# Norm roots through logarithm and exponential, and a head and a tail cut into feature blocks, in a two-layer decoder trunk

## The chip, the cores and the metric

The kernel runs on one core of a Trainium2 chip. Four engines work beside each other and meet only at semaphores: TensorE multiplies matrices and writes its sums to PSUM, ScalarE evaluates functions and copies, VectorE does elementwise arithmetic, and GpSimd does one elementwise operation here. SyncE's queue issues nearly all DMAs. The metric is device time in microseconds (us), from the start to the end of the program on the core. Lower is better.

## The reference

One inference step of a trunk of two layers, for a prompt of 1,024 tokens and 8 single-token samples, so 1,032 token columns of 1,024 features. A layer is, in float32:

```
x += RMSNorm_post([window attention ; HGRN2 recurrence](RMSNorm_pre(x) @ w_in) @ w_o)
x += RMSNorm_post(cross attention to 256 memory tokens(RMSNorm_pre(x)))
x += RMSNorm_post(gated MLP(causal depthwise conv(RMSNorm_pre(x) @ w_up)) @ w_down)

RMSNorm(x) = x * rsqrt(mean(x*x) + 1e-6) * g
memory keys, values = RMSNorm(mem_prompt) @ w_xk, w_xv
HGRN2 output: o = o * rsqrt(mean(o*o, over 128) + 1e-6) * gn * silu(gate), for each of 4 heads
```

It returns the 1,032 columns of x and the new caches.

## The kernel before, in words

Features lie on the 128 partitions in KT = 8 blocks, tokens in the free dimension. `xT` is the residual stream, `Y` the output of a sub-layer, `rs` the scale of a norm for each token. The tokens are cut into three chunks, of 344 columns in the mixer's projections and in the MLP, and of 384, 384 and 264 in the two stages between.

A float32 product is made of three fast ones (`mm3`, lines 256 to 260): each operand is split into a rounded high part and the remainder, as `hh` and `hl` for the activations and `w_hi` and `w_lo` for the weights. ScalarE makes the high parts, VectorE the low part of activations (L1094, L1103, L1639, L2499), and GpSimd the low part of a weight slab of 128x1024 (L243). From the end of the output projection to the query projection VectorE does this for 13 slabs per layer (L252, `low_slab`). Two raw and three split slabs are held, so each load waits for a split and each split waits for TensorE to have used an older slab. A "unit" is one slab times one chunk: 8 blocks of 3 matmuls.

There is no scheduler. The order on each engine is the order of the code, written out by hand in functions named `sync`, `gpsimd`, `tensor`, `scalar` and `vector`, and an instruction that waits holds back everything behind it on its engine. The stages of a layer:

1. Mixer (`stage_mixer`): 22 slabs by 3 chunks. The units of later slabs are spread as "hooks" through the recurrence of four heads. Each head ends with its norm: TensorE sums the squares of the output, 8 matmuls of one column at L944, ScalarE takes the square root (L1079), VectorE the reciprocal of 8 values per partition (L1317) and multiplies an identity by them (L1318), TensorE spreads these to all partitions (L951), VectorE multiplies (L1326). In the last head VectorE also applies the rotary embedding (`rope`, L1191 to L1193).
2. Window attention and the memory's projection (`stage_window`): 16 units `memory(f)` beside 16 groups of attention. `memory(0)` waits for all 8 blocks of the memory's low part `ml` (L637).
3. Output and query projection (`stage_output_query`), 4. cross attention (`stage_cross_ffn`), 5. the MLP. Its last two slabs run together with the norm after it (class `End`). In layer 0 that norm runs into the mixer of layer 1, in layer 1 into `stage_last`, which writes x out.

A norm of a chunk: squares (ScalarE), their sum over features (a matmul against `ones`), `Sqrt` (ScalarE, L299, L980, L1538, L1970, L2340), `RECIPROCAL` (VectorE, L1116, L1615, L1648, L1990, L2018, L2485, L2508), and for a post-norm a multiplication of the whole chunk (L1622, L1994, L2487) and the residual, which multiplies by the gain and adds to `xT` (L1629, and in `End` L2004: one instruction for each of the 8 blocks).

The start (`stage_start` and the first lines of the mixer): the DMA queue loads the first slab, then chunk 0 of x, the second slab, chunks 1 and 2, the constants and the memory, and after them the third slab. ScalarE and VectorE split chunk 0 in 8 blocks each, and the first unit waits for the last block.

## Time and profile before

| | us |
|---|---|
| median of three runs | 3418.66 (3417.93 to 3419.36) |
| profiled execution, its own time | 3425.52 |
| its span, first to last instruction | 3423.7 |
| TensorE busy in matmuls | 3237.8 (95%) |
| VectorE busy | 2308.0 (67%) |
| ScalarE busy | 1173.6 (34%) |
| GpSimd busy | 686.8 (20%) |

The mean granted clock of TensorE is 0.983 of full speed. Busy time of a matmul counts from its start to its modelled end, and neighbours overlap, so the times at which matmuls start say more than their lengths. An idle time in brackets at the end of a row is how long the engine had nothing before it, and the arrow names what it waited for.

### The profile page before, as it was taken

What the parts mean: (1) busy time and instruction counts of PE and PEld (TensorE: products, weight loads), DVE (VectorE), ACT (ScalarE), POOL (GpSimd) and SP (SyncE); (2) the same over time, 40 slices, a digit from 0 to 9 for tenths busy, and PEclk for the clock granted to TensorE, in tenths of its full rate; (3) what the DMA queues carried; (4) which work ended last, traced back from release to release, by engine and by line L of the source; (5) the groups of instructions that cost most, each with busy time, mean ns of one, the idle gap of its engine ahead of it and who ended that gap; (6) DMA issues with size and microseconds to landing.
All of it is one profiled execution on the core that took longest, in us unless ns stands there. A gap on an engine that the chain in (4) does not pass through costs nothing. (4 is left out here: it accounts for less than half of the span.)

```text
span 3423.7 us, 51853 instructions
## 1 busy us (share of the span) xinstructions
PE 3237.8 (95%) x21872; PEld 3075.0 (90%) x21872; DVE 2308.0 (67%) x3413; ACT 1173.6 (34%) x1849; POOL 686.8 (20%) x274
## 2 busy tenths in 40 slices
PE   7999889899899999999989998898999999999997
PEld 7998769788799999999879987798887999999996
DVE  6776782834677767676787776737355777777776
ACT  5442363434522222222344424533344222121212
POOL 1111131012322222222111111310133222222220
PEclk9999999999999999999999999999999999999998
DMA  5112233213411111111121122332053111111111
GB/s 179 45 39 69 71 94 124 74 43 143 175 44 50 44 50 44 50 44 50 49 83 39 51 63 77 112 112 72 28 192 127 44 56 39 55 44 50 44 54 52
DMA packets 80135, 245.87 MB, mean 72 GB/s; under 512 B 7968, under 2 KB 32800, under 8 KB 76064
## 3 DMA queue, kind: packets, MB, share of 16 engines
q1 hardware_dynamic: 79616, 242.50, 21.1%
q8 instruction: 173, 2.83, 0.3%
q14 instruction: 58, 0.48, 0.0%
q10 hardware_dynamic: 288, 0.06, 0.0%
HBM read 214.20 MB, written 23.04 MB: 69 GB/s over the span
## 5 line engine op out<-in xcount | busy, mean ns | idle before, releaser
L258 PE MATMUL ps<-hh,w_hi 128*128 128x344 f32 (+2 forms) x4320 | 1418.2, 328 | 84.5 <-DVE w_lo L252 27.9
L259 PE MATMUL ps<-hl,w_hi 128*128 128x344 f32 (+2 forms) x4320 | 1391.3, 322 | 0.0
L260 PE MATMUL ps<-hh,w_lo 128*128 128x344 f32 (+2 forms) x4320 | 1391.1, 322 | 0.0
L243 POOL TENSOR_TENSOR w_lo<-w_raw,w_hi 128x1024 fp32r<-128x1024 f32 x270 | 686.6, 2545 | 2674.3 <-ACT w_hi L235 2674.3
L258 PEld LDWEIGHTS ps<-hh,w_hi 128*128 128x128 f32 x4320 | 822.5, 190 | 113.1 <-issue 53.9
L259 PEld LDWEIGHTS ps<-hl,w_hi 128*128 128x128 f32 x4320 | 822.1, 190 | 3.1 <-issue 0.9
L260 PEld LDWEIGHTS ps<-hh,w_lo 128*128 128x128 f32 x4320 | 822.3, 190 | 0.0
L2608 DVE TENSOR_TENSOR Y<-Y,ps 128x344 f32<-128x344 f32 x912 | 433.1, 513 | 155.7 <-PE ps L260 155.7
L235 ACT ACTIVATE w_hi<-w_raw 128x1024 fp32r<-128x1024 f32 x296 | 310.6, 1052 | 440.0 <-PE ps L260 381.7
L2407 ACT ACTIVATE f_c<-f_u,cT 128x1032 f32<-128x1032 f32 (+1 forms) x92 | 111.4, 1213 | 635.0 <-DVE f_u L2573 628.4
L259 PE MATMUL ps<-f_glo,w_hi 128*128 128x344 f32 x960 | 308.0, 321 | 0.0
L260 PE MATMUL ps<-f_ghi,w_lo 128*128 128x344 f32 x960 | 307.9, 321 | 0.0
L258 PE MATMUL ps<-f_ghi,w_hi 128*128 128x344 f32 x960 | 306.0, 319 | 0.0
L2581 DVE SCALAR_TENSOR_TENSOR f_c<-f_u,cT,f_c 128x1024 f32<-128x1024 f32 x172 | 225.2, 1309 | 98.7 <-ACT f_c L2407 95.6
L258 PEld LDWEIGHTS ps<-f_ghi,w_hi 128*128 128x128 f32 x960 | 181.2, 189 | 0.0
L260 PEld LDWEIGHTS ps<-f_ghi,w_lo 128*128 128x128 f32 x960 | 180.5, 188 | 0.0
L259 PEld LDWEIGHTS ps<-f_glo,w_hi 128*128 128x128 f32 x960 | 180.3, 188 | 0.0
L2573 DVE TENSOR_TENSOR f_u<-ps,rs 128x1032 f32<-128x1032 f32 x86 | 105.7, 1230 | 63.5 <-PE ps L260 63.3
L2583 DVE SCALAR_TENSOR_TENSOR f_c<-f_cache,cT,f_c 128x8 f32<-128x8 f32 x172 | 124.1, 722 | 6.2
L1603 DVE TENSOR_TENSOR oq_acc<-oq_acc,oq_sq 128x384 f32<-128x384 f32 (+1 forms) x84 | 43.3, 515 | 96.3 <-ACT oq_sq L1528 92.4
L2423 ACT ACTIVATE f_ghi<-f_c 128x1032 fp32r<-128x1032 f32 x42 | 44.9, 1069 | 149.2 <-DVE f_c L2589 149.2
L1126 DVE TENSOR_TENSOR Y<-ps,rs 128x344 f32<-128x344 f32 x120 | 60.0, 509 | 47.6 <-PE ps L260 47.4
(357 smaller groups left out, 3717.5 us busy)
## 6 DMA issues: line engine op xcount, KB each, us to landing
w_raw<-in_w_stream SPq DMA_DIRECT2D x296, 512.0 KB, 3.5
out_y_cols<-xT SPq DMA_DIRECT2D x9, 1376.0 KB, 6.2
xT<-out_y_cols SPq DMA_DIRECT2D x2, 4128.0 KB, 13.6
mem_keys<-in_cache_mem_k SPq DMA_DIRECT2D x6, 1024.0 KB, 5.2
Y<-in_cache_mem_k SPq DMA_DIRECT2D x6, 1024.0 KB, 7.8
mem_values<-in_cache_mem_v SPq DMA_DIRECT2D x6, 1024.0 KB, 8.0
mem_keys<-in_cache_mem_v SPq DMA_DIRECT2D x6, 1024.0 KB, 7.8
xT<-in_x_cols SPq DMA_DIRECT2D x3, 1376.0 KB, 11.3
```

The source lines that it names most:

```text
L235: nc.scalar.activation(w_hi[:, SLOT[m], :], w_raw[:, m % RR, :], ACT.Copy).then_inc(hi_done, 1)
L243: nc.gpsimd.tensor_tensor(w_lo[:, SLOT[m], :], w_raw[:, m % RR, :], w_hi[:, SLOT[m], :].bitcast(F32), ALU.subtract).then_inc(lo_done["pool ...
L258: nc.tensor.matmul(out, whi, mhi, start=start, stop=False)
L259: nc.tensor.matmul(out, whi, mlo, start=False, stop=False)
L260: return nc.tensor.matmul(out, wlo, mhi, start=False, stop=stop)
L1126: nc.vector.tensor_tensor(dst[:, cols(c)], ps[:, u % 3, 0:CH], rs[:, cols(c)], ALU.mult)\
L2407: nc.scalar.activation(C[:, h, at], U[:, h, 2 + at.start:2 + at.stop], ACT.Identity, bias=cT[:, l, 3, col:col + 1], scale=cT[:, l, 2, col: ...
L2423: nc.scalar.activation(gh[:, j % 2, :], C[:, 1, :], ACT.Copy).then_inc(f_gh, 1)
L2573: nc.vector.tensor_tensor(tokens3(U[:, h, 2:2 + T]), ps[:, 3 * h:3 * h + 3, 0:CH], tokens3(rs[:]), ALU.mult).then_inc(f_up, 1)
L2581: dve_c(nc.vector.scalar_tensor_tensor(c[:, 0:SEQ], U[:, h, t:t + SEQ], w, c[:, 0:SEQ], ALU.mult, ALU.add))
L2583: dve_c(nc.vector.scalar_tensor_tensor(c[:, SEQ:T], ca[:, col, t, :], w, c[:, SEQ:T], ALU.mult, ALU.add))
L2608: nc.vector.tensor_tensor(y, y, b, ALU.add).then_inc(f_y, 1)
```

## The change

Roots. Everywhere a norm took `Sqrt` on ScalarE and `RECIPROCAL` on VectorE, ScalarE now makes the inverse root by two activations, `Ln` of the mean plus epsilon and `Exp` of minus half of that (`inverse_root`). The second waits for the first. VectorE only waits. The table set with both functions is loaded by name (`load_log_exp`) at the start, behind sigmoids and silus, and at the end of each MLP.

Head norms. The squares of a head are summed by `ones` as the stationary operand over 512 columns at a time, so the sum arrives on all partitions, and ScalarE takes the inverse root of 1,024 columns. The 8 one-column matmuls, the identity product and the second broadcast go. In the order of ScalarE, two exponentials of the next head now come ahead of the root.

End of an MLP. ScalarE multiplies `Y` by the gain in place, block by block, behind each square (`gained`). The multiplication by `rs` goes in two halves of 4 blocks, and the residual is a plain addition of 4 blocks at a time. x is written out in halves in `stage_last`, where ScalarE's root of chunk 1 now stands before three blocks of chunk 2.

Start. Chunk 0 of x arrives in two DMAs of 4 blocks, ScalarE and VectorE wait for the half that they need, VectorE and TensorE wait block by block, and the first mean comes behind the second unit. `memory(0)` waits for its operand block by block.

```diff
+        def load_log_exp():
+            nc.scalar.preload_act_table_set("natural_log_exp_and_others")
+        def inverse_root(out, log, total, n, ready):
+            act_c(nc.scalar.activation(log, total, ACT.Ln, bias=epst[:], scale=1.0 / n))
+            nc.scalar.activation(out, log, ACT.Exp, scale=-0.5).then_inc(ready, 1)
...
+                def x_here(self, eng, c, k=KT - 1):
+                    if c == 0 and k < KT // 2:
+                        eng.wait_ge(x_half, 16)
+                    else:
+                        eng.wait_ge(x_in[c], 16)
...
-                sp.dma_start(xT[chunk(0)], io["x_cols"][chunk(0)]).then_inc(x_in[0], 16)
+                sp.dma_start(xT[:, 0:4, 0:CH], io["x_cols"][:, 0:4, 0:CH]).then_inc(x_half, 16)
+                sp.dma_start(xT[:, 4:KT, 0:CH], io["x_cols"][:, 4:KT, 0:CH]).then_inc(x_in[0], 16)
...
                             for k in range(KT):
+                                if f == 0:
+                                    pe.wait_ge(s["m_lo"], k + 1)
...
-                        pe.wait_ge(s["m_lo"], KT)
                         memory(0)
...
-                            if end and w == 0:
-                                pe.wait_ge(end.s["hl"], KT * c + k + 1)
+                            if w == 0:
+                                pe.wait_ge((end.s if end else s)["hl"], KT * c + k + 1)
...
                         unit(0)
+                        unit(1)
                         mean_of_x(0)
-                        for u in (1, 2, 3):
+                        for u in (2, 3, 4):
...
-                        for c in range(NB):
-                            nc.tensor.matmul(ps[:, BB, c:c + 1], att[:, P * c:P * c + P], ones[:, 0:1], start=True, stop=True)
+                        for h in range(2):
+                            nc.tensor.matmul(ps[:, BB + h, :], ones[:], att[:, 512 * h:512 * h + 512], start=True, stop=True)
...
-                        unit(hook_units(r, 11)[0])
-                        pe.wait_ge(s["spread"], r + 1)
-                        for h in range(2):
-                            last = nc.tensor.matmul(ps[:, BB + h, :], ones[:], RT[:, 512 * h:512 * h + 512],
-                                                    start=True, stop=True)
-                        last.then_inc(s["cast"], 1)
-                        for u in hook_units(r, 11)[1:]:
-                            unit(u)
+                        hook(r, 11)
...
-                        nc.scalar.activation(sq8[:], ps[:, BC, 272:272 + NS], ACT.Sqrt, bias=epst[:],
-                                             scale=1.0 / P).then_inc(s["root"], 1)
                         if more:
                             exp_level(r + 1, 1)
                             exp_level(r + 1, 2)
+                        act.wait_ge(s["mean"], r + 1)
+                        inverse_root(two(RT), two(RT), pair(BB), P, s["root"])
+                        inverse_root(sq8[:], sq8[:], ps[:, BC, 272:272 + NS], P, s["root"])
...
-                        nc.vector.tensor_tensor(two(y[:, 0:SEQ]), two(y[:, 0:SEQ]), pair(BB), ALU.mult)\
-                            .then_inc(s["normed"], 1)
+                        nc.vector.tensor_tensor(y[:, 0:SEQ], y[:, 0:SEQ], RT, ALU.mult).then_inc(s["normed"], 1)
...
                             nc.scalar.activation(self.slot(e, k), Y[:, k, cols3(c)], ACT.Square).then_inc(self.s["sq"], 1)
+                            nc.scalar.activation(Y[:, k, cols3(c)], Y[:, k, cols3(c)], ACT.Copy,
+                                                 scale=gT[:, l, G_POST_FFN + k:G_POST_FFN + k + 1]).then_inc(self.s["gained"], 1)
...
-                        dve_c(nc.vector.reciprocal(rs[:, cols3(c)], rs[:, cols3(c)]))
...
+                        for h in range(2):
+                            at = (slice(None), slice(4 * h, 4 * h + 4), cols3(c))
+                            nc.vector.tensor_tensor(Y[at], Y[at], over_heads(rs[:, cols3(c)], 4), ALU.mult)\
+                                .then_inc(self.s["norm"], 1)
...
+                            nc.vector.tensor_tensor(xT[at], xT[at], Y[at], ALU.add).then_inc(self.s["x"], 1)
...
+                    for h in range(2):
+                        sp.wait_ge(end.s["x"], 2 * c + h + 1)
+                        at = (slice(None), slice(4 * h, 4 * h + 4), slice(CH * c, CH * c + CH))
+                        sp.dma_start(io["y_cols"][at], xT[at]).then_inc(y_out, 16)
```

VectorE at the end of a head, before. `hg_blast` holds the 8 roots, `xT` the spread scale, `Y<-ps,rs` is the evacuation of a unit:

```order
L1126 TENSOR_TENSOR Y<-ps,rs 128x344
L1317 RECIPROCAL hg_blast<-hg_blast 128x8
L1318 TENSOR_TENSOR xT<-ident,hg_blast 128x1024
L1320 RECIPROCAL hg_sq<-hg_sq 128x8
L1321 TENSOR_TENSOR Y<-Y,hg_sq 128x8
L1162 TENSOR_TENSOR hg_work<-hg_work,xT 128x512
L1164 TENSOR_TENSOR hg_work<-hg_work,xT 128x512
L1126 TENSOR_TENSOR Y<-ps,rs 128x344
L1326 TENSOR_TENSOR Y<-Y,ps 128x1024
```

The same place now:

```order
L1135 TENSOR_TENSOR Y<-ps,rs 128x344
L1171 TENSOR_TENSOR hg_work<-hg_work,xT 128x512
L1173 TENSOR_TENSOR hg_work<-hg_work,xT 128x512
L1328 TENSOR_TENSOR Y<-Y,hg_sq 128x8
L1135 TENSOR_TENSOR Y<-ps,rs 128x344
L1330 TENSOR_TENSOR Y<-Y,xT 128x1024
```

The reciprocals and the identity product are gone, and the two products of the next head stand ahead of the wait for the root. ScalarE at the same place, before (L1004 is the exponential of the next head's levels):

```order
L1075 ACTIVATE hg_work<-ps 128x1024
L1079 ACT_TABLE_LOAD
L1079 ACTIVATE hg_blast<-ps,epst 128x8
L1080 ACTIVATE hg_sq<-ps,epst 128x8
L1004 ACT_TABLE_LOAD
L1004 ACTIVATE hg_work<-hg_work 128x1024
L1004 ACTIVATE xT<-xT 128x1024
```

And now, where L1013 is that exponential:

```order
L1088 ACTIVATE hg_work<-ps 128x1024
L1013 ACTIVATE hg_work<-hg_work 128x1024
L1013 ACTIVATE xT<-xT 128x1024
L268 ACTIVATE xT<-ps,epst 128x1024
L269 ACTIVATE xT<-xT 128x1024
L268 ACTIVATE hg_sq<-ps,epst 128x8
L269 ACTIVATE hg_sq<-hg_sq 128x8
```

Two table loads have gone from here, and two activations of 1,024 columns have come, behind the exponentials. VectorE's last rows of the program, before:

```order
L1986 TENSOR_TENSOR Y<-Y,ps 128x344 x5
L1990 RECIPROCAL rs<-rs 128x344
L1994 TENSOR_TENSOR Y<-Y,rs 128x8x344
L2004 SCALAR_TENSOR_TENSOR xT<-Y,gT,xT 128x344 x8
L1990 RECIPROCAL rs<-rs 128x344
L1994 TENSOR_TENSOR Y<-Y,rs 128x8x344
L2004 SCALAR_TENSOR_TENSOR xT<-Y,gT,xT 128x344 x8
```

And now:

```order
L1984 TENSOR_TENSOR Y<-Y,ps 128x344 x5
L1993 TENSOR_TENSOR Y<-Y,rs 128x4x344 x2
L2004 TENSOR_TENSOR xT<-xT,Y 128x4x344 x2
L1993 TENSOR_TENSOR Y<-Y,rs 128x4x344 x2
L2004 TENSOR_TENSOR xT<-xT,Y 128x4x344 x2
```

Twenty rows of work have become thirteen. In the whole program ScalarE's order holds 64 table loads before and 44 now, and no norm root has one directly ahead of it.

## Rows read from the trace of the kernel before

**Rows 1.** The page, part 1: engine, busy us, share of the span, instructions.

```profile
PE 3237.8 (95%) x21872; PEld 3075.0 (90%) x21872; DVE 2308.0 (67%) x3413; ACT 1173.6 (34%) x1849; POOL 686.8 (20%) x274
```

**Rows 2.** Busy time of each engine by stretch; PEclk is the granted clock.

```profile
core 0: us, PE busy (x) PEld busy (x) DVE busy (x) ACT busy (x) POOL busy (x), PEclk, DMA share, GB/s
...
586.00:672.00 86.00, 70.74 (x423) 66.87 (x422) 72.20 (x100) 42.51 (x80) 0.00 (x0) 0.94 0.25 80
...
1671.00:1754.00 83.00, 66.92 (x324) 58.14 (x323) 71.37 (x92) 35.38 (x61) 10.11 (x4) 0.89 0.22 77
```

**Rows 3.** Groups in both mixers, PE: count, busy us, mean ns, idle before, releaser.

```profile
L944 PE MATMUL ps<-ones,hg_work 128*128 128x1 f32 x128 | 14.7, 245 | 0.0
```

**Rows 4.** The end of a head; start us, length, engine, line, idle before.

```profile
76.36 1.09 PE L901 MATMUL ps<-ident,Y 128*128 128x128 f32 x8 [0.95 <-DVE Y L1126]
...
215.92 1.88 PE L951 MATMUL ps<-xT,ones 128*128 128x512 f32 x4
...
219.20 2.02 PE L852 MATMUL ps<-hg_set 128*128 128x128 f32 x16 [0.42 <-DVE Y L1326]
...
214.13 1.06 ACT L1004 ACTIVATE hg_work<-hg_work 128x1024 f32<-128x1024 f32 x1
```

**Rows 5.** Output and query projection of layer 0, the same columns.

```profile
634.59 2.56 DVE L1648 RECIPROCAL rs<-oq_rt 128x384 f32<-128x384 f32 x1 [0.18 <-ACT oq_rt L1538]
...
641.51 0.44 PE L258 MATMUL ps<-hh,w_hi 128*128 128x384 f32 x1 [2.13 <-DVE w_lo L252]
...
645.68 1.80 DVE L1615 RECIPROCAL oq_rt<-oq_rt 128x264 f32<-128x264 f32 x1
...
653.76 0.69 PE L258 MATMUL ps<-hh,w_hi 128*128 128x384 f32 x1 [3.46 <-DVE w_lo L252]
```

**Rows 6.** The last head's end and the memory's first unit.

```profile
385.48 1.98 PE L951 MATMUL ps<-xT,ones 128*128 128x512 f32 x4 [1.80 <-DVE xT L1318]
...
401.70 1.28 ACT L542 ACT_TABLE_LOAD   x1
...
402.50 0.58 PE L258 MATMUL ps<-mem_hi,w_hi 128*128 128x256 f32 x1 [4.28 <-DVE mem_lo L637]
```

**Rows 7.** From the MLP of layer 0 into the mixer of layer 1.

```profile
1725.37 2.30 DVE L1990 RECIPROCAL rs<-rs 128x344 f32<-128x344 f32 x1
...
1733.61 3.98 DVE L2004 SCALAR_TENSOR_TENSOR xT<-Y,gT,xT 128x344 f32<-128x344 f32 x8
...
1733.84 1.49 PE L1928 MATMUL ps<-e_whole,ones 128*128 128x344 f32 x2 [3.82 <-DVE e_whole L2013]
```

**Rows 8.** The tail of the program.

```profile
3397.30 4.79 PE L1922 MATMUL ps<-e_squares,ones 128*128 128x344 f32 x16
...
3399.00 2.30 DVE L1990 RECIPROCAL rs<-rs 128x344 f32<-128x344 f32 x1 [0.99 <-ACT rs L1970]
...
3404.40 3.99 DVE L2004 SCALAR_TENSOR_TENSOR xT<-Y,gT,xT 128x344 f32<-128x344 f32 x8
...
3413.69 3.99 DVE L2004 SCALAR_TENSOR_TENSOR xT<-Y,gT,xT 128x344 f32<-128x344 f32 x8
```

**Rows 9.** The head of the program.

```profile
9.37 3.88 ACT L963 ACTIVATE hh<-xT,gT 128x344 fp32r<-128x344 f32 x8 [2.81 <-DMA xT<-in_x_cols]
...
13.39 6.09 DVE L1094 SCALAR_TENSOR_TENSOR hl<-xT,gT,hh 128x344 fp32r<-128x344 f32 x8 [8.88 <-ACT hh L963]
...
19.63 0.63 PE L258 MATMUL ps<-hh,w_hi 128*128 128x344 f32 x1 [19.63 <-DVE hl L1094]
...
24.40 1.06 ACT L235 ACTIVATE w_hi<-w_raw 128x1024 fp32r<-128x1024 f32 x1 [7.81 <-DMA w_raw<-in_w_stream]
...
25.53 2.39 POOL L243 TENSOR_TENSOR w_lo<-w_raw,w_hi 128x1024 fp32r<-128x1024 f32 x1 [8.87 <-ACT w_hi L235]
```

**Rows 10.** The page, part 6: DMA, KB each, median us to landing.

```profile
w_raw<-in_w_stream SPq DMA_DIRECT2D x296, 512.0 KB, 3.5
...
out_y_cols<-xT SPq DMA_DIRECT2D x9, 1376.0 KB, 6.2
```

More of the change, by code:

```diff
@@ L298, in root @@
                     act.wait_ge(s["mean"], 1)
[L299 removed]
+                    inverse_root(mrs[:], mrs[:], ps[:, 7, 0:NMEM], D, s["root"])
                 def scale(self, dve):
                     dve.wait_ge(s["root"], 1)
[L303 removed]
             def sync(sp):
@@ L810, in unit @@
                             wait_low(pe, m)
-                        if w < 3 and not end:
-                            pe.wait_ge(s["hl"], c + 1)
                         if u >= 3:
@@ L1198, in vector @@
                         end.tree(dve, 2)
-                        end.residual(dve, 1, range(KT))
+                        end.residual(dve, 1, (0, 1))
                         end.scale(dve, 2)
@@ L1205, in vector @@
                         end.tree(dve, 4)
-                        end.residual(dve, 2, range(KT))
+                        end.residual(dve, 2, (0, 1))
                         end.scale(dve, 4)
@@ L1533, in root @@
                         def root(i):
+                            kind, c = MEANS[i]
                             act.wait_ge(mean_ready, i + 1)
-                            if i >= 2:
-                                act.wait_ge(rt_used, i - 1)
-                            n = C3[MEANS[i][1]][1]
-                            nc.scalar.activation(rt[:, i % 2, 0:n], ps[:, 3, 0:n], ACT.Sqrt, bias=epst[:], scale=1.0 / D)\
-                                .then_inc(rt_ready, 1)
+                            if i >= 2 and MEANS[i - 2][0] == "post":
+                                act.wait_ge(rt_used, sum(k == "post" for k, _ in MEANS[:i - 1]))
+                            r = rt[:, i % 2, 0:C3[c][1]]
+                            inverse_root(r if kind == "post" else rs[:, cols(c)], r, ps[:, 3, 0:C3[c][1]], D, rt_ready)
                         def high(c):
@@ L1866, in stage_cross_ffn @@
                     EVENTS += [("pre", 0), ("post", 2), ("pre", 1), ("pre", 2)] if l + 1 < DEPTH else [("post", 2)]
-                    s = {n: sem(f"e_{n}") for n in ("sq", "sum", "root", "x", "hh", "hl", "rs", "norm", "whole", "tree", "mean")}
+                    s = {n: sem(f"e_{n}") for n in ("sq", "gained", "sum", "root", "x", "hh", "hl", "norm", "whole", "tree", "mean")}
                     added = 24 * (FT - 2)
@@ L2335, in root @@
                     def root(i):
+                        kind, c = MEANS[i]
                         act.wait_ge(s["mean"], i + 1)
-                        if i >= 2:
-                            act.wait_ge(s["rt_used"], i - 1)
-                        w = C3[MEANS[i][1]][1]
-                        nc.scalar.activation(rt[:, i % 2, 0:w], ps[:, mean_bank(i), 0:w], ACT.Sqrt, bias=epst[:], scale=1.0 / D)\
-                            .then_inc(s["root"], 1)
+                        if i >= 2 and MEANS[i - 2][0] == "post":
+                            act.wait_ge(s["rt_used"], sum(k == "post" for k, _ in MEANS[:i - 1]))
+                        r = rt[:, i % 2, 0:C3[c][1]]
+                        inverse_root(r if kind == "post" else rs[:, cols(c)], r, ps[:, mean_bank(i), 0:C3[c][1]], D, s["root"])
                     def high(c, ks):
@@ L2682, in scalar @@
                 end.scalar(act)
-                end.squares(act, 2, range(KT))
+                end.squares(act, 2, range(5))
                 end.root(act, 1)
+                end.squares(act, 2, range(5, KT))
                 end.root(act, 2)
@@ L2689, in vector @@
                 for c in (1, 2):
-                    end.normalise(dve, c)
-                    end.residual(dve, c, range(KT))
-                dve.wait_ge(end.s["x"], KT * NCH)
+                    end.reciprocal(dve, c)
+                    end.multiply(dve, c)
+                    end.residual(dve, c, (0, 1))
+                dve.wait_ge(end.s["x"], 2 * NCH)
             return Programs(sync, gpsimd, tensor, scalar, vector)
```

111 lines of the change are left out of this document (41 added, 70 removed).

## The prediction

> **What bounds the kernel now.** I read the engine shares first. TensorE is busy for 95% of the span [rows 1]. So a gain has to come from its own work or from the places where it stands still, and I listed its idle times above half a microsecond in the timeline, with what ended each. They sit in six kinds of places: the head, the ends of heads, the entry into the window stage, the stretch of the two projections, the norm between the layers, and the tail. In the projections VectorE is the busier engine, 72.20 of 86 us against TensorE's 70.74, and between the layers 71.37 of 83 against 66.92 [rows 2]. There TensorE waits for VectorE's chain, and a reciprocal in that chain is on the path. In the long MLPs TensorE has hardly an idle time, and nothing that the change does there reaches the path. All sums below are made against the profiled execution. Its span is 3423.7, its own time 3425.5, and the median of the runs 3418.7. A saving is taken over in full to the median.
>
> **Head ends, 8.4 us.** The 128 one-column matmuls cost 14.7 us of TensorE with no idle time ahead of them [rows 3], 1.84 for each of 8 heads. They go. The two 512-column matmuls (1.88 us) remain and move into their place, four microseconds earlier. They used to cover the evacuation of the last unit before the next head's transposes. That cover is gone. The price is shown where there never was a cover: 0.95 us before L901 after three evacuations [rows 4]. Here one is left, so I take 0.8. The wait of 0.42 before L852, which is for VectorE's multiplication of the norm, goes, since the bank is now free once ScalarE has read it. For a change of heads that is 1.84 + 0.42 - 0.8, about 1.4, and there are six: 8.4 us. ScalarE does more: two activations of 1,024 columns at about 1.06 each [rows 4] in place of two small ones, so the root is ready some 2.7 us after the sum. The unit behind the sum takes TensorE about 4 us and the transposes about 1.1 [rows 4], so this is hidden, by about 2.5 us. Were it not, TensorE would wait at L852 and everything behind it.
>
> **Last head and window, 7.2 us.** In each layer's last head the idle time of 1.80 before L951, behind VectorE's rotation and identity product, goes with the wait [rows 6], and 1.84 us of small matmuls too. But the last evacuation stands behind the last rotation, which waits for a DMA that VectorE starts when the rotation before it ends, and that order stays. I estimate 2.1 us there. Next, `memory(0)` started 4.28 us late, after all 8 low parts [rows 6]. Now it starts after the first. The table load of 1.28 us ahead of the window's first exponential goes. What is late next is the second group's probabilities on VectorE, and they leave 1.5 of these. So 3.6 per layer.
>
> *A rule beside it.* The load takes 1.28 us [rows 6]. The Trainium skill (ScalarE: Activation LUTs, What ACT_TABLE_LOAD costs) states that each switch of sets costs a drain of about 1.38 us besides, about 2.66 us in all. By that, the two loads on the window's path would be worth about 2.8 us more. The row has the load alone, nothing in the trace shows a drain, and I keep to the row.
>
> **Projections, 7.5 us.** TensorE waits for the low part of a slab three times here, 2.13 and 3.46 us being two of the waits [rows 5], and in front of the slabs stand three reciprocals, of which 2.56 and 1.80 us are two; the first has the length of the second. The first, for post-norm 0, gives nothing: the slab behind it is not split before then, and the largest wait of the stretch hangs on ScalarE's order. Those of post-norm 1 and pre-norm 0 move VectorE by 2.2 us, since the query's scale cannot come before TensorE's sum; the last adds 1.8. Less the new activation, TensorE meets the next wait (3.46) about 3.75 us earlier. Twice 3.75 is 7.5.
>
> **Cross attention, 0.5 us.** The samples' caches arrive by DMA and set the pace. Earlier normalisation takes a little contention from the splits of the slabs, about 0.8 per layer, and the last root, on which TensorE waits before the third chunk of the MLP's first slab, is longer by one activation, about 0.5. Net 0.5 in all.
>
> **Between the layers, 6 us.** Four reciprocals of 2.30 are on VectorE's chain, and two residuals of 3.98 [rows 7]. Multiplying a chunk takes 3.1 (from 3399.00 + 2.30 to 3404.40 [rows 8]), and an addition of the same 2,752 columns should take the same, 0.9 less than the eight fused ones. Against this, ScalarE now makes two activations for each block: at 0.485 a block (3.88 for 8) [rows 9] the eight squares of chunk 0 end about 3 us later. TensorE works on those for 4.8 us anyhow, so it loses about 1.9, and the first scale comes 1.5 later than with the reciprocal. Followed through the three sums, the start of the fourth unit comes 2 us earlier, the sum at 1733.84 about 4, and the last sum 6 to 8. I take 6.
>
> **Tail, 9 us.** From 3399.00 to the span's end VectorE and the last output are alone: 2.3 + 3.1 + 4.0, the same again, and 6.0 for the last DMA (3413.69 + 3.99 to 3423.7) [rows 8]. Now the root of chunk 1 is made before the last blocks arrive, so multiplication starts when the last addition ends, about 3398.0 (TensorE is done at 3397.30). Four pieces of 3.1 end at 3410.4. The root of chunk 2 needs TensorE's sum (3397.30 + 4.79 = 3402.1) and two activations, 3403.2, and the multiplication wants it at 3404.2: in time. A DMA of 512 KB lands in 3.5 us, one of 1,376 KB in 6.2 [rows 10], so 688 KB less save 2.1. The end is at 3410.4 + 3.9 = 3414.3. That is 9.4; I take 9, for ScalarE's longer rows.
>
> **Head, 2.3 us.** TensorE's first product was at 19.63, after 8 high parts (9.37, 3.88) and 8 low parts (13.39, 6.09) one after the other [rows 9]. With half of chunk 0 landed some 2 us sooner (half of 1,376 KB, by the price above) and a wait per block, it starts at about 9, when the first slab is split. That looks like 10 us, but the third slab lands at 24.40 and is split at 25.53 + 2.39 = 27.9 whatever happens before, because the DMA queue is unchanged. TensorE will do two units and stop. The third cannot start before that. What remains, estimated between 1 and 3, is 2.3 us; the cleared reciprocal of 2.30 keeps the fourth from waiting.
>
> *A rule beside it.* VectorE's low parts of chunk 0 took 6.09 us for 8 with a split on GpSimd beside them, against 3.98 for 8 fused instructions of that width between the layers [rows 9, 7]. The Trainium skill (SBUF - State Buffer, Who interferes with whom) calls the pair of ports that both use an exclusive lock for the whole instruction. By it, the low parts of chunk 1, which now start under the split at 25.53, wait for it, and the head's gain would shrink to about 1.
>
> **The rivals.**
> (a) The clock comes back too. Granted clock was 0.94 in the projections of layer 0 and 0.89 between the layers [rows 2], some 14 us of half speed's loss, behind stops that now get shorter; two thirds more of the kind lie elsewhere. If a third of it is returned, 8 to 10 us more: about 3368. For it: the low clock follows the stops. Against: most stops are only shortened, and the head gets a new one.
> (b) ScalarE is late. If squares with gains and the long roots each cost more than I allow, between the layers brings 1 and the head ends 3, the rest as above: 9 less of the gain and 2 to 4 at other roots, about 3390.
> (c) Slower than before. ScalarE's extra 2 us per head delays the split of a slab, and TensorE waits for slabs in place of norms. It decides once a split falls later than the start of its unit, more than 5 us after now; then each of 32 slabs in heads would cost up to 2 us, 64 less 41: about 3442. Against: ScalarE is idle for two thirds of the time there, and TensorE shows no wait for a split in the heads.
> (d) The change does not do what it says: table loads come back ahead of each `Ln`. The order of ScalarE shows 44 loads, none at a root, so little speaks for it. Price: 1.28 at some 40 roots, half of them on the path, 26 us: about 3403.
>
> **How the numbers follow.** 8.4 + 7.2 + 7.5 + 0.5 + 6 + 9 + 2.3 is 40.9, so 3418.7 becomes 3378. Chances: this case 0.60, (a) 0.16, (b) 0.18, (d) 0.03, (c) 0.03. Adding the bounds of the terms (tail 7 to 10, between the layers 3 to 9, head 1 to 3, head ends 5 to 10, the rest by a third either way), the range is 3364 to 3394, which takes in (a) and (b). A measurement of this kernel can tell 0.2%, about 7 us, from no change. Only (c) lies on the slow side, and little of (d) and of what I have not seen lies near no change: faster 0.96, same 0.01, slower 0.03.
>
> **What would show it.** Right: the last residual ends near 3370 of a span of about 3383, with an end 14 us after TensorE's last sum begins; L901 shows idle times of 0.6 to 0.9 at changes of heads and L852 none; the first product stands near 9, followed by a stop of about 8 us before the third slab; waits for slabs in the projections fall by some 4 us per layer. Wrong: the head shows 8 us or more of gain, TensorE waits for ScalarE's root at a change of heads, the clock is 1.00 where it was 0.89, or the sum of idle times between the layers has not fallen.

## The result, and the profile after

The changed kernel takes 3380.97 us (median of 4 runs, 3377.77 to 3383.46) against 3418.3 us of the kernel before on the same chip: a ratio of 0.9890, 95% interval 0.9873 to 0.9907. On the chip of the first experiments it came to 3379.54 us and 0.9877 (0.9863 to 0.9890). The forecast was 3378 with a range from 3364 to 3394. It held in its sum; several of its terms were off, and some of them cancel. One execution of one kernel below, heads as before, took 6381.9 us, nothing like any other run, and its ratio leaves it out.

The profiled execution has a span of 3381.7 us, 42.0 less than the one before. The medians lie 37.3 apart: the profiled execution of the kernel before was 7 us above its median, that of the changed kernel 2.5. Part 1 of its page, in the columns of [rows 1]:

```profile
PE 3220.8 (95%) x21744; PEld 3057.6 (90%) x21744; DVE 2222.3 (66%) x3322; ACT 1202.9 (36%) x1928; POOL 677.4 (20%) x274
```

TensorE has 17 us less to do (128 matmuls fewer and less of it at half clock), VectorE 86 us less, ScalarE 29 us more. To see where the 42 us came from I took the start of the same instruction in both timelines at each border of a stage; the differences add up to the span's. Forecast is the prediction's term, with layers 0 and 1 apart. The second profile is one more execution of the changed kernel, from the first experiments.

```
stage (us)                                            before   after   second profile   change   forecast
program's start to the first transposes                 76.4    75.6    75.6             -0.7      -2.3
three changes of heads, layer 0                        212.2   209.7   208.1             -2.5      -4.2
fourth head to the window's transposes, layer 0        104.9   102.7   102.0             -2.1      -2.1
window's transposes to its last memory unit, layer 0   114.8   115.6   114.1             +0.9      -1.5
end of window, both projections, layer 0               217.8   213.4   213.2             -4.4      -3.8
cross attention, first slab of the MLP, layer 0        252.1   250.5   251.3             -1.6      -0.2
rest of the MLP, layer 0                               694.1   694.3   694.3             +0.2       0
between the layers (to the first transposes)           101.6    91.7    89.6             -9.9      -6
three changes of heads, layer 1                        215.3   208.1   208.1             -7.2      -4.2
fourth head to the window's transposes, layer 1        104.0   102.9   102.7             -1.1      -2.1
window's transposes to its last memory unit, layer 1   114.7   114.9   112.9             +0.2      -1.5
end of window, both projections, layer 1               219.4   215.4   214.1             -4.0      -3.8
cross attention, first slab of the MLP, layer 1        253.2   252.2   250.8             -1.0      -0.2
MLP, layer 1, to TensorE's last matmul                 721.2   721.8   721.5             +0.6       0
TensorE's last matmul to the span's end                 22.1    12.7    12.7             -9.4      -9
```

How far such a stage can be trusted shows in the last two profiles, which are of one kernel: 10.7 us apart. The head that begins at 214 takes 71 us in the one and 69 in the other, with the same 601 matmuls and the same idle time. Busy time by stretch, in the columns of [rows 2], of the first profile:

```profile
214.00:285.00 71.00, 70.25 (x601) 65.92 (x601) 54.14 (x85) 30.91 (x32) 9.53 (x4) 0.98 0.14 47
...
1661.00:1754.00 93.00, 82.93 (x437) 73.68 (x437) 66.41 (x90) 62.88 (x103) 14.86 (x6) 0.94 0.25 86
```

and of the second:

```profile
214.00:283.00 69.00, 68.69 (x601) 64.36 (x601) 53.70 (x84) 30.92 (x32) 9.53 (x4) 1.00 0.15 48
...
1658.00:1749.00 91.00, 80.16 (x438) 70.89 (x437) 66.80 (x89) 62.40 (x102) 14.63 (x6) 0.98 0.25 88
```

The granted clock is 0.98 in the one and 1.00 in the other: one stretch of 3.4 us at 1.2 GHz in place of 2.4 costs TensorE 1.55 us here (70.93 against 69.38 from transposes to transposes). Up to TensorE's last matmul the three profiles have 99 (before), 89 and 58 us at 1.2 GHz. A difference of 1.5 or 3 us in a single stage of a single profile may be only that. So below I look at idle times as well as at lengths.

**Changes of heads.** The timeline of TensorE at the end of the second head, the place of [rows 4]:

```profile
207.85 1.88 PE L962 MATMUL ps<-hg_work,ones 128*128 128x512 f32 x4
209.56 0.28 PE L964 MATMUL ps<-hg_sq,ones 128*128 128x8 f32 x2
...
214.40 1.09 PE L919 MATMUL ps<-ident,Y 128*128 128x128 f32 x8 [0.68 <-DVE Y L1135]
...
215.44 1.73 PE L870 MATMUL ps<-hg_set 128*128 128x128 f32 x14
```

The column sums are gone, the idle time behind the evacuation is 0.68 (forecast 0.8), and the products behind the transposes start without one.

**Window.** TensorE at the place of [rows 6], then ScalarE:

```profile
388.06 1.94 PE L532 MATMUL ps<-ident,xT 128*128 128x128 f32 x8 [4.20 <-PEq L369]
...
395.18 0.55 PE L258 MATMUL ps<-mem_hi,w_hi 128*128 128x256 f32 x1 [2.09 <-DVE mem_lo L655]
...
403.25 0.66 PE L488 MATMUL ps<-ident,xT 128*128 128x128 f32 x4 [1.62 <-DVE xT L644]
```

```profile
394.01 3.30 ACT L586 ACTIVATE mem_hi<-mem_values,gT 128x256 fp32r<-128x256 f32 x8 [2.94 <-DMA mem_values<-in_mem_cols]
397.21 0.39 ACT L560 ACTIVATE xT<-xT,win_small 128x129 f32<-128x129 f32 x1
```

The wait of 4.28 is 2.09 now. But ScalarE's high parts wait for the memory's data until 394.01, the window's exponentials stand behind them on ScalarE, and TensorE waits 1.62 (with 0.43 ahead of it) for the probabilities they lead to. The three add up to 4.14 (3.51 in layer 1, where one wait of 4.14 stood before). And the idle time ahead of the window's transposes, 4.20 now, was 2.19:

```profile
393.43 1.50 PE L513 MATMUL ps<-ident,xT 128*128 128x128 f32 x8 [2.19 <-PEq L352]
```

The wait of 1.80 ahead of the last head's broadcast [rows 6] has gone, and this one is 2.0 longer. In the kernel with heads as before, below, the two are 1.79 and 2.19 again.

**Between the layers.** TensorE's stops at the place of [rows 7], then ScalarE ahead of them:

```profile
1689.70 0.42 PE L258 MATMUL ps<-hh,w_hi 128*128 128x344 f32 x1 [1.36 <-DVE hl L1114]
1692.30 0.66 PE L258 MATMUL ps<-hh,w_hi 128*128 128x344 f32 x1 [1.86 <-DVE hl L1114]
...
1719.61 0.82 PE L1925 MATMUL ps<-e_whole,ones 128*128 128x344 f32 x2 [1.55 <-DVE e_whole L2011]
...
1731.75 0.82 PE L1925 MATMUL ps<-e_whole,ones 128*128 128x344 f32 x2 [2.31 <-DVE e_whole L2011]
```

```profile
1661.58 0.48 ACT L1950 ACTIVATE e_squares<-Y 128x344 f32<-128x344 f32 x1
1661.96 0.57 ACT L1951 ACTIVATE Y<-Y,gT 128x344 f32<-128x344 f32 x1
```

The wait of 3.82 for the second sum [rows 7] is 1.55. Counted from the start of the stage, this sum comes 4.0 us earlier and the last one 8.2. All idle time of the stage went from 17.3 to 10.1 us. Square and copy alternate at 0.85 us a block, and TensorE's sum of squares goes at that pace.

**Tail.** VectorE and ScalarE at the place of [rows 8]:

```profile
3365.30 3.09 DVE L1993 TENSOR_TENSOR Y<-Y,rs 128x1376 f32<-128x1376 f32 x2
3368.31 3.09 DVE L2004 TENSOR_TENSOR xT<-xT,Y 128x1376 f32<-128x1376 f32 x2
...
3371.31 3.09 DVE L1993 TENSOR_TENSOR Y<-Y,rs 128x1376 f32<-128x1376 f32 x2
3374.32 3.09 DVE L2004 TENSOR_TENSOR xT<-xT,Y 128x1376 f32<-128x1376 f32 x2
```

```profile
3369.50 0.55 ACT L268 ACTIVATE rs<-ps,epst 128x344 f32<-128x344 f32 x1 [2.89 <-PE ps L1919]
3370.08 0.49 ACT L269 ACTIVATE rs<-rs 128x344 f32<-128x344 f32 x1
```

Four pieces of 3.09 without a pause, the last root done at 3370.57, before VectorE wants it at 3371.31. From TensorE's last sum (3364.67) to the end are 17.0 us; the prediction's sum had 3414.3 - 3397.3 = 17.0.

**Head.** TensorE, ScalarE's neighbour VectorE and GpSimd, at the place of [rows 9]:

```profile
18.43 0.66 PE L258 MATMUL ps<-hh,w_hi 128*128 128x344 f32 x1 [18.43 <-DMA lvl_mask<-in_c_lvl]
...
75.64 1.10 PE L919 MATMUL ps<-ident,Y 128*128 128x128 f32 x8 [2.96 <-DVE Y L1135]
```

```profile
69.50 0.69 DVE L1164 TENSOR_TENSOR hg_work<-hg_set 128x512 f32<-128x512 f32 x1
70.22 2.76 DVE L1165 TENSOR_TENSOR hg_work<-hg_set 128x512 f32<-128x512 f32 x1
```

```profile
70.02 2.42 POOL L243 TENSOR_TENSOR w_lo<-w_raw,w_hi 128x1024 fp32r<-128x1024 f32 x1 [1.79 <-ACT w_hi L235]
```

The first product waits for the constants' DMA, not for data, and 2.96 us of idle time stand ahead of the first transposes.

### The profile page after: what moved, and what is told of

Read it like the earlier page. It is cut to its first block and busy times, and to the rows that moved or that the text cites. A ratio compares the mean times of both kernels' runs of the same rounds, so it can differ in the third digit from the quotient of the medians.

```text
span 3381.7 us, 51592 instructions
## 1 busy us (share of the span) xinstructions
PE 3220.8 (95%) x21744; PEld 3057.6 (90%) x21744; DVE 2222.3 (66%) x3322; ACT 1202.9 (36%) x1928; POOL 677.4 (20%) x274
## 5 line engine op out<-in xcount | busy, mean ns | idle before, releaser
L243 POOL TENSOR_TENSOR w_lo<-w_raw,w_hi 128x1024 fp32r<-128x1024 f32 x270 | 677.2, 2510 | 2650.5 <-ACT w_hi L235 2650.5
```

The lines of the kernel that those rows point to most:

```text
L243: nc.gpsimd.tensor_tensor(w_lo[:, SLOT[m], :], w_raw[:, m % RR, :], w_hi[:, SLOT[m], :].bitcast(F32), ALU.subtract).then_inc(lo_done["pool ...
```

## The experiments

Eleven edits of the changed kernel, with the changed kernel itself beside the first three. Ratios are to the kernel before on the same chip.

**The changed kernel again.** 

> The changed kernel once more, on the chip of the three kernels below and in five rounds, so that each of them can be set against it. Both theories: 37 us below the kernel before, give or take 2 us.

3379.54 us, 0.9877 (0.9863 to 0.9890): 39 us below.

**Reciprocals back.**

```diff
-            nc.scalar.activation(out, log, ACT.Exp, scale=-0.5).then_inc(ready, 1)
+            nc.scalar.activation(out, log, ACT.Exp, scale=0.5).then_inc(ready, 1)
...
+                        dve_c(nc.vector.reciprocal(x, x))   # wherever VectorE waits for a root
```

> The changed kernel with every wide reciprocal back on VectorE: ScalarE's second activation gives the root (power 0.5 in place of -0.5), VectorE inverts it where it waits for it. The logarithms, halves, unit order and heads stay. Theory 1 (the reciprocals stood on VectorE's chain and TensorE waited for them): about 21 us come back, 7.5 in the two projection stretches, 8 to 9 between the layers, 4.6 in the tail behind TensorE's last sum, 1 in the cross attention, under 1 before the first transposes. Theory 2 (the reciprocals were hidden and the gain is the clock's and the other edits'): under 8 us in all, and idle times of TensorE in the projections as in the changed kernel.

3415.19 us, 0.9985 (0.9977 to 0.9994): 36 us come back, all but 4 of the gain, and more than theory 1's 21. By stage, against the second profile: projections 5.2 and 6.2, between the layers 13.8, head 5.8, tail 4.7 and 2.8 ahead of it, cross attention 2.5 and 0.8. The tail's two inversions are exactly its two times 2.3:

```profile
3393.83 2.29 DVE L273 RECIPROCAL rs<-rs 128x344 f32<-128x344 f32 x1
3396.16 3.10 DVE L2002 TENSOR_TENSOR Y<-Y,rs 128x1376 f32<-128x1376 f32 x2
...
3402.18 2.30 DVE L273 RECIPROCAL rs<-rs 128x344 f32<-128x344 f32 x1
```

Between the layers the busy times are

```profile
1673.00:1778.00 105.00, 85.83 (x440) 76.13 (x440) 82.90 (x95) 61.95 (x101) 13.76 (x6) 0.92 0.22 76
```

with 19.2 us of idle time in place of 10.8, and a clock of 0.92 where the same stage had 0.98. So the 13.8 are 8.4 of waiting, which is theory 1's 8 to 9, and 5.4 that go with the clock. This kernel is not the one before in these places: it has the second activation and the reciprocal one behind the other, and is slower there than before (103.4 against 101.6; head 81.3 against 76.4). So its 36 us are not the reciprocals' share of the gain: with the next two kernels' 15 and 6 they would make 57 of 39. That the reciprocals were on TensorE's path is shown, and theory 2 falls.

**Heads as before.**

```diff
-                        for h in range(2):
-                            nc.tensor.matmul(ps[:, BB + h, :], ones[:], att[:, 512 * h:512 * h + 512], start=True, stop=True)
+                        for c in range(NB):
+                            nc.tensor.matmul(ps[:, BB, c:c + 1], att[:, P * c:P * c + P], ones[:, 0:1], start=True, stop=True)
...
+                        pe.wait_ge(s["spread"], r + 1)
```

> The changed kernel with only the norm of the heads as before: 128 one-column products, the product with the identity on VectorE, and the wait of the second group of products for it (the roots still by logarithm, on 8 columns). Theory 1 (TensorE's own work and two waits went): 1.4 us for each of six changes of heads and 2.1 for each of the two last heads, 12.6 us in all, the idle time ahead of the first transposes of a head below 0.1 again. Theory 2 (the gain at the changes of heads is the table loads' and the clock's): under 5 us.

3394.85 us, 0.9921 (0.9906 to 0.9936): 15 us. Behind the second and third transposes of a layer a head without a stretch at half clock takes 70.94 here and 69.38 in the changed kernel, 1.56 more; behind the first, where the wait of 0.42 never stood, it took 70.34 in the kernel before, 0.96 more. The last heads are 3.8 and 1.4 us longer, of which 1.5 in layer 0 is a longer wait for an evacuation in the middle of the head. The place of [rows 4] reads as before:

```profile
218.22 1.88 PE L969 MATMUL ps<-xT,ones 128*128 128x512 f32 x4
219.94 1.04 PE L919 MATMUL ps<-ident,Y 128*128 128x128 f32 x8
...
221.50 0.68 PE L870 MATMUL ps<-hg_set 128*128 128x128 f32 x4 [0.42 <-DVE Y L1340]
```

Theory 1, which said 12.6; four of the heads also have one stretch at half clock each here, and none has one in the second profile.

**Edges as before.**

```diff
-                                if f == 0:
-                                    pe.wait_ge(s["m_lo"], k + 1)
+                        pe.wait_ge(s["m_lo"], KT)       # ahead of memory(0)
...
-                end.squares(act, 2, range(5))
+                end.squares(act, 2, range(KT))
                 end.root(act, 1)
...
+                        sp.dma_start(io["y_cols"][:, :, at], xT[:, :, at])   # whole chunks
```

> The changed kernel with its edges as before: chunk 0 used only when both halves are there and TensorE waits for all eight low parts, the memory's first unit waits for all low parts, each output chunk leaves whole, and the last root but one comes after all eight squares. Theory 1 (each of these edits pays on its own): about 3 us more in the tail, 1 to 3 in each window stage, 1 to 2 in the head, 7 to 10 in all. Theory 2 (in the head the third slab, and in the window the exponentials behind the memory's high parts, set the time whatever TensorE waits for): the tail's 3 us and under 1 us for the rest.

3385.47 us, 0.9896 (0.9882 to 0.9909): 6 us. The tail is 3.8 longer. The first transposes come at 75.3, not later than in the changed kernel: in the head theory 2 holds. From the window's transposes to its last memory unit it is 2.4 and 2.7 us longer, but its idle time is 15.1 against 14.4 and 13.9 against 13.6: the wait itself is worth under 1 us in a layer. The rest goes with the clock: 12 us at half clock in both, where the second profile has 6 and 5.

**TensorE kept busy in the stops.**

```diff
+            for _ in range(n):
+                nc.tensor.matmul(ps[:, bank, 0:P], ones[:], ones[:], start=True, stop=True)
```

> The changed kernel with idle time of TensorE filled by products of ones whose result nobody reads: 9 and 14 ahead of the waits for the second and third trees between the layers, 30 ahead of the last unit of the output projection and 9 and 15 ahead of the seventh and eighth unit of the query projection, 0.14 us each. Theory 1 (a stop costs its own length and then a stretch at half clock, 1.55 us lost for each 3.4 us of it): the stretches at half clock in the projections and between the layers go from 10 to 17 us per stage to under 4, and 4 to 8 us come off the median. Theory 2 (the clock falls whatever TensorE does in the stops): the same stretches at half clock, and the time between no change and 2 us more, for products that last beyond a stop.

3380.19 us, 0.9888 (0.9871 to 0.9904): nothing gained. In the projections of layer 0 the idle time fell from 15.6 to 7.1 and the time at half clock from 13.7 to 3.4 us, and the stretch took 212.4 in place of 213.2; in layer 1 the idle time fell from 18.3 to 8.6, the half clock stayed at 10.2, and it took 216.8 in place of 214.1. Neither theory has both. The idle products in the projections lasted longer than the stops they fill. The 30 of them ahead of the last unit of the output projection (60 records):

```profile
599.32 6.86 PE L265 MATMUL ps<-ones 128*128 128x128 f32 x60
605.93 0.37 PE L258 MATMUL ps<-hh,w_hi 128*128 128x264 f32 x1
```

They take 6.6 us, for a stop of 5.42 in the second profile, and TensorE goes on behind them without idle time, as behind the other two groups of the stretch. Together the three take 11.8 us. Idle time and idle products are 18.9 us in layer 0, 3.3 more than the 15.6 of the second profile, and the stretch is still 0.8 shorter: the 10.3 us less at half clock gave back about 4 (an estimate from these figures; 1.55 for 3.4 us would be 4.7). In layer 1 the sum is 20.4 against 18.3, the half clock the same, and the stretch 2.6 longer. Between the layers it is 13.5 against 10.8, the half clock 3.4 us in both, and the stage 91.9 in place of 89.6. So the lost time at half clock is real here too, and products fitted to the stops more closely were not tried. Each figure is of one profile.

**Two orders turned.**

```diff
                         self.squares(act, 0, range(KT))
+                        self.gains(act, 0, range(KT))
...
+                        exps(0)
                         act.wait_ge(s["mem_in"], 16)
...
-                        exps(0)
                         exps(1)
```

> The changed kernel with two orders turned. Between MLP and norm ScalarE makes all eight squares of chunk 0 and then its eight copies with gain. In the window stage its first exponentials stand ahead of the memory's high parts, and VectorE divides the first group by its sum between the fourth and fifth low part. Theory 1 (TensorE's sum of squares runs at the pace of ScalarE's square and copy, 6.1 us in place of 4.8, and the window's first probabilities wait behind the memory's data): the sums take 4.8 us again, 1.3 less in each layer, and about 1 us goes from the idle time behind the memory's first unit in each window stage, 4 to 5 us in all. Theory 2 (what TensorE gains there it waits at the next norm and at the second group's probabilities): sums of 4.8 us and under 1.5 us in all.

3378.28 us, 0.9877 (0.9862 to 0.9892). TensorE's sum of squares in the changed kernel and then in this one:

```profile
1661.92 6.14 PE L1919 MATMUL ps<-e_squares,ones 128*128 128x344 f32 x16
```

```profile
1658.88 4.89 PE L1920 MATMUL ps<-e_squares,ones 128*128 128x344 f32 x16 [0.20 <-ACT e_squares L1951]
```

In the window ScalarE's first exponential starts before the memory's data is there, and 1.6 and 0.8 us of idle time go:

```profile
390.57 0.41 ACT L560 ACTIVATE xT<-xT,win_small 128x129 f32<-128x129 f32 x1 [1.80 <-DVE win_small L637]
...
392.38 3.30 ACT L587 ACTIVATE mem_hi<-mem_values,gT 128x256 fp32r<-128x256 f32 x8
```

Both places moved as theory 1 says. The total cannot decide: 0.9877 is the ratio of the changed kernel on one chip, and 4 us below its 0.9890 on the other. Idle time between the layers is 11.5 in place of 10.8, with 10.2 us at half clock in place of 3.4; one profile can't say whether the stages behind or the clock took the gain back.

**The head, one edit at a time.** A: the constants' wait moved.

```diff
-                pe.wait_ge(s["consts"], 32)
...
+                        pe.wait_ge(start.s["consts"], 32)    # behind unit 8
```

> The changed kernel with one wait moved: TensorE waits for the constants before the first transposes, not before its first product. The prediction's step on the head (the third slab lands and is split at 28 whatever comes before it) expects the first product at 10 to 11, a stop before the third slab, and the first transposes where they were, within 1 us. The rival (the wait for the constants held back the whole head): first transposes 5 us earlier or more.

3380.55 us, 0.9884 (0.9868 to 0.9899). The timeline of TensorE:

```profile
10.25 0.63 PE L258 MATMUL ps<-hh,w_hi 128*128 128x344 f32 x1 [10.25 <-DVE hl L1107]
```

```profile
28.41 0.66 PE L258 MATMUL ps<-hh,w_hi 128*128 128x344 f32 x1 [7.22 <-POOL w_lo L243]
```

```profile
76.06 1.09 PE L920 MATMUL ps<-ident,Y 128*128 128x128 f32 x8 [2.96 <-DVE Y L1136]
```

Eight microseconds earlier at the first product, 7.22 us of stop before the third slab, and nothing at the first transposes: the prediction's step.

B: the same, and the third slab ahead of chunk 2 of x.

```diff
+                load_slabs(sp, RR + 1)
                 sp.dma_start(xT[chunk(2)], io["x_cols"][chunk(2)])
```

> The same, and the third slab's transfer ahead of chunk 2 of x. If the third slab is what the head waits for, TensorE's stop goes, and the first transposes come 3 to 8 us earlier. If ScalarE's gates and the sums before them set the time of the first transposes, less than 2 us, and the idle time ahead of them grows to 5 us or more.

3374.96 us, 0.9860 (0.9844 to 0.9877). No stop at the third slab, first transposes at 66.87, 8.7 earlier than in the changed kernel, above the 3 to 8 expected, with the same 2.96 ahead of them.

C: the sum of chunk 2 a unit earlier, the memory's mean and root behind the gates.

```diff
-                        for u in (5, 6, 7):
+                        for u in (5, 6):
                             unit(u)
                         mean_of_x(2)
-                        start.mean(pe)
+                        unit(7)
                         unit(8)
+                        start.mean(pe)
```

> The changed kernel with the sum of squares of chunk 2 one unit earlier and the memory's mean and root behind the gates; constants and slabs as they were. If the gates set the time of the first transposes, the 2.96 us ahead of them go to under 1, and they come 2 to 3 us earlier. If not, under 0.5 us.

3375.54 us, 0.9869 (0.9854 to 0.9884). First transposes at 73.10, 2.5 earlier:

```profile
73.10 1.09 PE L920 MATMUL ps<-ident,Y 128*128 128x128 f32 x8 [0.61 <-DVE Y L1138]
```

All three together: 

> The changed kernel with another head: TensorE waits for the constants before the first transposes and not before its first product, the third slab's transfer stands ahead of chunk 2 of x, the third sum of squares is one unit earlier and the memory's mean and root are behind the gates. Theory 1 (the wait for the constants kept the first product at 18.5, the third slab and then the gates kept the rest): first product at 10 to 11, first transposes 4 to 7 us earlier. Theory 2 (VectorE's work from the first low parts to the last evacuation is what the head lasts, whatever comes earlier): first product at 10 to 11, first transposes less than 1.5 us earlier.

3368.52 us, 0.9849 (0.9834 to 0.9863). First product at 11.4, first transposes at 65.74, 9.8 us earlier, idle time in between 0.6: the head is TensorE's own work now. Theory 1, with more than it said.

**Both.** 

> The two kernels before this one together: head, squares before copies, and exponentials before the memory's high parts. The sum of what the two bring: by theory 1 of each 8 to 12 us below the changed kernel, by theory 2 of each under 3.

3366.15 us (3365.33 to 3366.79), 0.9841 (0.9826 to 0.9856): 12 to 17 us below the changed kernel by the two ratios that it has, and with the next one the fastest of all. The head alone was 2.4 above it.

**The last slab's splits moved.**

```diff
-                    split_hi(act, fits_after(VISIT[l, "mem", 0] - 1))
+                    split_hi(act, fits_after(VISIT[l, "mem", 0] - 1) - 1)
...
+                        split_hi(act, fits_after(VISIT[l, "mem", 0] - 1))    # start of the window stage
```

> The last kernel (head, squares before copies, exponentials first) and one more edit: the last slab's two splits of a mixer are made at the start of the window stage, where VectorE is idle, and not beside VectorE's last product of the last head, which took 2.74 us with the split beside it and 1.22 in the heads before. Theory 1 (VectorE waits for GpSimd's split): that product takes 1.22, the idle time of 4.2 us ahead of the window's transposes falls to about 2.7, and 2 to 3 us go in all. Theory 2 (the idle time is that of the rotation's transfer and of the change of stage): the product is shorter and the idle time stays above 3.7, no change within 1 us.

3367.0 us, 0.9840 (0.9826 to 0.9853): no change. VectorE and GpSimd in the changed kernel (second profile), then VectorE here:

```profile
378.23 2.74 DVE L1330 TENSOR_TENSOR Y<-Y,xT 128x1024 f32<-128x1024 f32 x1
```

```profile
377.49 2.40 POOL L243 TENSOR_TENSOR w_lo<-w_raw,w_hi 128x1024 fp32r<-128x1024 f32 x1 [8.52 <-ACT w_hi L235]
```

```profile
367.57 1.22 DVE L1337 TENSOR_TENSOR Y<-Y,xT 128x1024 f32<-128x1024 f32 x1
369.88 1.23 DVE L1207 TENSOR_TENSOR Y<-Y,hg_set 128x1032 f32<-128x1032 f32 x1 [1.10 <-DMA hg_set<-Y]
```

The product is 1.5 us shorter, and VectorE then waits 1.10 for the rotation's transfer; the idle time ahead of the window's transposes is 3.86. Theory 2.

## Why the prediction was right or wrong, by its steps

The number came out right in part by luck. Window and head were to bring 5.3 us and cost 0.4 together; more than forecast between the layers, in the projections and in the cross attention made up for it, and part of that is the clock's. The range was also stated 1 to 2 us wider than its bounds add up to (3366 to 3393).

**Head ends (8.4).** Right. Without half clock the three stretches of a layer go from 70.34 + 70.94 + 70.94 to three times 69.38, which is 4.1 us and 8.2 in all; the wait of 0.42 behind the third change stood in the fourth head's stretch and has gone too, so 9.0. The forecast's terms are there, with an idle time of 0.68 for the 0.8. ScalarE's long rows stayed hidden. That the stage sums read 2.5 and 7.2 in one profile is half clock, which fell once in a head after, and twice in heads of layer 1 before.

**Last head and window (7.2).** The last head was near: 2.1 and 1.1 measured, 2.9 and 1.3 in the second profile, for 2.1 in each, with the 0.42 just named in them. But this is the small products' 1.84 and not the wait of 1.80, which moved ahead of the window's transposes. The window was wrong: the step that said "what is late next is the second group's probabilities on VectorE, and they leave 1.5 of these" left about nothing. Next late are ScalarE's high parts, which wait for the memory's data (2.94 us of idle time), with the exponentials behind them on the same engine. The wait I removed and the one I priced in its place both hang on that one transfer. Idle time in this stretch was 14.4 before and 14.6 after in layer 0. The row that shows this DMA as ScalarE's releaser was there before; I read only what ended TensorE's wait.

**Projections (7.5) and cross attention (0.5).** The mechanism was right, since putting the reciprocals back brings the waits back, and the sizes were off. The projections became 8.3 and 9.8 us shorter in the two profiles, but their idle time fell by only 2.4 and 3.7 in the two layers, 6.1 for the 7.5 forecast; the waits for slabs behind the first fell by 2.2 and 3.0 and not by some 4. The rest goes with the clock. The cross attention became 2.6 and 3.2 shorter, and its idle time fell from 16.1 to 14.3 and from 15.7 to 14.1: 3.4 us in place of 0.5.

**Between the layers (6).** The waiting was right: 7.3 us less idle, less 1.3 for the sum of squares that goes at ScalarE's pace (the prediction had 1.9 there), is 6.0. The stage gained 9.9, and in the second profile 12.0. The difference goes with the granted clock, 0.89 before, 0.94 and 0.98 after: 20.5 us at half clock before, 10.2 and 3.4 after.

**Rival (a)**, the clock returns too, at 0.16, was therefore half true, and my choice between it and the main case was not an either-or. It filled part of what the window and the head did not bring: 10 us less at half clock in the first profile, 41 in the second, at 1.55 for 3.4 us some 5 and 19 us (an estimate, since the stretches partly fall into idle time). That a stretch at half clock costs time on its own is shown in the heads, and the kernel with idle products fits the same price in the projections.

**Tail (9).** Right: 9.4, and 17.0 us from the last sum to the end as worked out. Two of the markers I gave for it were wrong by my own sum: it gives 17 us behind the start of the last sum and a last residual that ends near 3379 of 3383, not 14 and 3370. Measured are 17.0 and 3377.4 of 3381.7.

**Head (2.3).** The step "the third slab is split at 27.9 whatever happens before" was right and decided it; edit A shows it. Two others failed. "It starts at about 9" overlooked the first line of TensorE's program, a wait for 32 counts of the constants, which was covered before by 8 low parts and lasts to 18.4 (edit A). And what remained, 2.7 us at the fourth unit, did not reach the first transposes: only 0.7 did. The sums of squares moved one unit back and the memory's root became two activations, so the gates start at 59.8 where they had been at 58.4, and VectorE loses 2 us beside a split of GpSimd. Edit C takes the first of these away and gains 2.5. I took the gain at the fourth unit over to the end of the head without following VectorE through it.

The rule I weighed there, that VectorE and GpSimd hold their pair of ports one at a time (the Trainium skill, SBUF — State Buffer, Who interferes with whom), fits the rows: a VectorE product of 0.69 us takes 2.76 when GpSimd's split of 2.42 is under way, one of 1.22 takes 2.74, and without the split it is 1.22 again. The low parts of chunk 1, which the prediction named, took 5.68 us behind the split at 26.17 where they had taken 3.99. The fourth unit still came 2.7 earlier. The other rule, a drain of about 1.38 us besides each table load (the Trainium skill, ScalarE: Activation LUTs, What ACT_TABLE_LOAD costs), is not borne out by the rows. In the window of the kernel before, the load at 401.70 [rows 6] stands between these two of ScalarE:

```profile
398.38 3.30 ACT L568 ACTIVATE mem_hi<-mem_values,gT 128x256 fp32r<-128x256 f32 x8 [2.39 <-DMA mem_values<-in_mem_cols]
...
403.00 0.41 ACT L542 ACTIVATE xT<-xT,win_small 128x129 f32<-128x129 f32 x1
```

The high parts end at 401.68 and the load at 402.98, so 0.02 us are left on either side; 43 of the 64 loads are followed as closely. The first row is also the DMA that I did not read. That the window did not gain says nothing of the rule, since its path went by that DMA.

**Rivals (b), (c), (d).** ScalarE was late in one place, the sum of squares, for 1.3 us (b). No slab of a head was late (c), and no load came back (d).

## What to carry to other kernels

A wait that goes has a next one behind it, and it is found by following every engine that feeds the waiting one, down to the DMA that it waits for, not by the idle times of the bounding engine alone. When work at the program's head is made earlier, read each engine's first wait in the code: one that was covered has no row in the profile. The largest part of the gain, 21 of 42 us in the projections, the cross attention and between the layers, and 4.6 in the tail, came with taking reciprocals of 1.7 to 2.6 us, 37 in the program, off a chain on which another engine waits, though the clock has a share in it. The largest one left lay in the order of the first transfers.

## What the runs showed of the hardware that was not expected

Two executions of the changed kernel have spans of 3370.9 and 3381.7 us, with 58 and 89 us at 1.2 GHz; a stretch of 3.4 us there costs a head 1.55. With the stops filled by idle products the time at half clock was 10 us less in the projections of one layer and the same in those of the other. And the eight scans of a head take 2.63 us alone (in the kernel with all three head edits) and 4.80 where a split of GpSimd stood beside them.
